# Norm weights applied to the transposed x, as a scale of its high and low parts, and first loads in halves

## The reference

```python
def rms_norm(x, g):
    y = x32 * lax.rsqrt(jnp.mean(x32 * x32, axis=-1, keepdims=True) + EPS)
    return (y * g).astype(x.dtype)

x = x + 0.5 * swiglu_ffn(x, ffn1_norm, ffn1_w_in, ffn1_w_out)   # D_FF = 5632
h = rms_norm(x, mix_norm)
proj = h @ w_in                                                 # six parts: q, k, v for A and for B
...                       # per-head norms, rotary, 8 dilated heads, 8 differential heads
x = x + mixed @ w_out
x = x + 0.5 * swiglu_ffn(x, ffn2_norm, ffn2_w_in, ffn2_w_out)
```

## Time and profile before

| | us |
|---|---|
| median of 3 runs | 1875.55 (1874.54 to 1876.12) |
| the profiled execution, whole | 1874.67 |
| its span in the profile | 1872.9 |
| PE busy | 1851.4 (99% of the span) |
| DVE busy | 1271.5 (68%) |
| ACT busy | 936.4 (50%) |

### The profile page before, as it was taken

One profiled execution on the slowest core, in us unless ns is written; L12 is line 12 of the kernel. 1 busy time (PEld: TensorE's weight loads), 2 busy tenths in 40 slices (PEclk: granted clock), 3 DMA queues, 4 the chain that ended last, 5 costly groups with the idle time before them and its releaser, 6 DMA issues.

```text
span 1872.9 us, 23158 instructions
## 1 busy us (share of the span) xinstructions
PE 1851.4 (99%) x8408; PEld 1531.9 (82%) x8408; DVE 1271.5 (68%) x1432; ACT 936.4 (50%) x1167; POOL 60.1 (3%) x60
## 2 busy tenths in 40 slices
PE   7999999999999999999999999999999999999999
PEld 6888888888888888877888788888888888888887
DVE  6777788778754554668777667688877887744443
ACT  5455555555543444555555555555555555533432
POOL 0000000000000000222021100000000000000000
PEclk9999999999999999999999999999999999999999
DMA  8555555555655555554545445455555555555563
GB/s 291 189 191 209 192 199 205 193 188 179 231 196 175 184 196 198 188 181 135 180 157 180 135 157 180 157 200 198 207 197 206 183 209 191 201 180 180 193 212 113
DMA packets 178137, 352.88 MB, mean 188 GB/s; under 512 B 6561, under 2 KB 7201, under 8 KB 177825
## 3 DMA queue, kind: packets, MB, share of 16 engines
q1 hardware_dynamic: 177936, 352.07, 54.7%
q10 hardware_dynamic: 144, 0.07, 0.0%
HBM read 350.01 MB, written 2.10 MB: 188 GB/s over the span
## 4 chain that ended last, share of the span: by engine, by line
PE 94%; DVE 3%; ACT 1%; issue 1%; POOL 1%; DMA 1%; SPq 0%; ACTq 0%
PE acc L376 21%; PE acc L378 20%; PE acc L377 20%; PE acc L480 6%; PE acc L481 6%; PE acc L479 6%; PE turn L419 2%; PE turn L420 2%; PE turn L418 2%; DVE w_lo L874 2%; PE turn L403 1%; PE acc L420 1%; PE acc L418 1%; PE acc L419 1%; PE turn L531 1%
## 5 line engine op out<-in xcount | busy, mean ns | idle before, releaser
L874 DVE TENSOR_TENSOR w_lo<-w_raw,w_hi 128x1024 fp32r<-128x1024 f32 x352 | 428.8, 1229 | 392.4 <-ACT w_hi L634 390.5
L634 ACT ACTIVATE w_hi<-w_raw 128x1024 fp32r<-128x1024 f32 x352 | 357.6, 1020 | 461.9 <-PE acc L378 440.2
L648 ACT ACTIVATE w_hi<-w_raw 128x1024 fp32r<-128x1024 f32 (+1 forms) x400 | 402.9, 1017 | 363.7 <-PE acc L481 131.5
L883 DVE TENSOR_TENSOR w_lo<-w_raw,w_hi 128x1024 fp32r<-128x1024 f32 (+1 forms) x400 | 460.6, 1169 | 151.9 <-ACT w_hi L648 146.3
L376 PE MATMUL acc<-w_hi,h_hi 128*128 128x512 f32 x992 | 392.4, 396 | 1.9 <-DVE w_lo L874 1.9
L378 PE MATMUL acc<-w_hi,h_lo 128*128 128x512 f32 x992 | 387.5, 391 | 0.0
L377 PE MATMUL acc<-w_lo,h_hi 128*128 128x512 f32 x992 | 387.3, 390 | 0.0
L376 PE MATMUL acc<-w_hi,act_hi 128*128 128x512 f32 x704 | 278.0, 395 | 0.0
L378 PE MATMUL acc<-w_hi,act_lo 128*128 128x512 f32 x704 | 276.0, 392 | 0.0
L377 PE MATMUL acc<-w_lo,act_hi 128*128 128x512 f32 x704 | 273.7, 389 | 0.0
L376 PEld LDWEIGHTS acc<-w_hi,h_hi 128*128 128x128 f32 x992 | 186.8, 188 | 42.1 <-issue 4.9
(11 more groups left out here) (133 smaller groups left out, 1571.7 us busy)
## 6 DMA issues: line engine op xcount, KB each, us to landing
w_raw<-in_ffn_w_in SPq DMA_DIRECT2D x176, 1024.0 KB, 4.9
w_raw<-in_ffn_w_out SPq DMA_DIRECT2D x64, 1024.0 KB, 5.0
w_raw<-in_w_in SPq DMA_DIRECT2D x48, 1024.0 KB, 5.1
w_raw<-in_ffn_w_out SPq DMA_DIRECT2D x32, 768.0 KB, 4.2
w_raw<-in_w_out SPq DMA_DIRECT2D x16, 1024.0 KB, 5.0
x_sb<-in_x SPq DMA_DIRECT2D x4, 512.0 KB, 7.9
out_y<-x_sb SPq DMA_DIRECT2D x4, 512.0 KB, 6.4
gain_row<-in_ffn_norm SPq DMA_DIRECT2D x4, 256.0 KB, 8.6
```

The lines of the kernel that those rows point to most:

```text
L634: nc.scalar.activation(w_hi[:, v % RING, 0:count, :], w_raw[:, v // 2 % RAW, k0:k0 + count, :], ACT.Copy).then_inc(hi_ready, 1)
L648: nc.scalar.activation(w_hi[:, v % RING, 0:count, :], w_raw[:, piece % RAW, k0:k0 + count, :], ACT.Copy).then_inc(hi_ready, 1)
L874: nc.vector.tensor_tensor(w_lo[:, v % RING, 0:count, :], w_raw[:, v // 2 % RAW, k0:k0 + count, :], w_hi[:, v % RING, 0:count, :].bitcast(F32),
L883: nc.vector.tensor_tensor(w_lo[:, v % RING, 0:count, :], w_raw[:, piece % RAW, k0:k0 + count, :], w_hi[:, v % RING, 0:count, :].bitcast(F3 ...
```

## The change

The norm weights are no longer broadcast. ACT's queue loads the three vectors as 48 rows of 128 (`norm_in`), PE transposes them once, and ACT copies them into `norm_gain`, one value per partition and tile. PE transposes x itself (`turn_x`, `turn_norm`), and the weight is applied while the result is split: ACT copies with a scale (`turn_norm_hi`), DVE forms x times weight minus the high part (`norm_lo`). As the scale differs from tile to tile, a group of 512 columns takes four instructions of 256 elements on each of the two engines, instead of one of 1024. `gain_x`, `gain_row` and its loads are gone, six in number. The first 256 columns of x and the first two tiles of weights are loaded by themselves, before the rest of their groups. Group 1 is transposed after unit 0, group 2 after unit 2, group 3 after unit 4. The squares of x are later in ACT's stream, and `down` is written out for its four chunks in place of a loop.

```diff
-            for c in range(4):
+            first = gate_up1[:, 0:UK, 0:NC], gate_up1[:, UK:2 * UK, 0:NC]
+            sp.dma_start(x_sb[:, :, 0:NC // 2], x_dram[:, :, 0:NC // 2]).then_inc(x_half_landed, 16)
+            sp.dma_start(w_raw[:, 0, 0:UK, :], first[0]).then_inc(first_landed, 16)
+            sp.dma_start(x_sb[:, :, NC // 2:NC], x_dram[:, :, NC // 2:NC]).then_inc(x_landed[0], 16)
+            sp.dma_start(w_raw[:, 0, UK:2 * UK, :], first[1]).then_inc(raw_landed[0], 16)
+            for c in range(1, 4):
                 cols = slice(c * NC, (c + 1) * NC)
                 sp.dma_start(x_sb[:, :, cols], x_dram[:, :, cols]).then_inc(x_landed[c], 16)
-                sp.dma_start(gain_row[:, cols], ffn1_norm[:, cols].to_broadcast([P, NC])).then_inc(x_landed[c], 16)
-                if c:
-                    load(gate_up1, 0, KT * (c - 1), KT, c - 1)
-            load(gate_up1, 0, KT * 3, KT, 3)
+                load(gate_up1, 0, KT * c, KT, c)
...
+            def turn_x(c, pair, split, ks=range(4)):
+                if split is not None:
+                    pe.wait_ge(turn_split, split)
+                for k in ks:
+                    for t in range(TT):
+                        at = c * NC + k * P
+                        mm = nc.tensor.transpose(turn4[pair][:, k, t * P:(t + 1) * P], x_sb[:, t, at:at + P], ident)
+                return mm
...
-                    chunk(PARTS_D, u0, range(1), h, 0, r0 - 4)
-                    turn_rows(r0 - 2, xg_at[2], r0 - 3)
-                    chunk(PARTS_D, u0, range(1, 4), h, 0, r0 - 4)
+                    pe.wait_ge(half_split, 1)
+                    chunk(PARTS_D, u0, range(1), h, 0)
+                    pe.wait_ge(x_landed[1], 16)
+                    turn_norm(1, xg_at[1], None)
+                    pe.wait_ge(turn_split, 1)
+                    chunk(PARTS_D, u0, range(1, 3), h, 0, r0 - 4)
+                    pe.wait_ge(x_landed[2], 16)
+                    turn_norm(2, xg_at[2], r0 - 3)
+                    chunk(PARTS_D, u0, range(3, 5), h, 0, r0 - 4)
+                    pe.wait_ge(x_landed[3], 16)
+                    turn_norm(3, xg_at[3], r0 - 2)
+                    chunk(PARTS_D, u0, range(5, 8), h, 0, r0 - 4)
...
+            def turn_norm_hi(n, r, c, pair):
+                act.wait_ge(rows_turned, r + 1)
+                for k in range(4):
+                    s = nc.scalar.activation(h_hi[:, 4 * c + k, :], turn4[pair][:, k, :], ACT.Copy,
+                                             scale=norm_gain[:, n, 4 * c + k:4 * c + k + 1])
+                s.then_inc(turn_hi, 1)
...
+            def norm_lo(n, c, pair, ks):
+                for k in ks:
+                    at = 4 * c + k
+                    s = nc.vector.scalar_tensor_tensor(h_lo[:, at, :], turn4[pair][:, k, :], norm_gain[:, n, at:at + 1],
+                                                       h_hi[:, at, :].bitcast(F32), ALU.mult, ALU.subtract)
+                return s
...
-            for c in range(2):
-                dve.wait_ge(x_landed[c], 32)
-                gain_x(ROWS[R_NORM1] + c, c, 0)
...
+            norm_lo(0, 0, xg_at[0], range(0, 2)).then_inc(half_split, 1)
+            split_lo(IN1, 0, 1, PARTS_D)
+            dve.wait_ge(turn_hi, 1)
+            norm_lo(0, 0, xg_at[0], range(2, 4)).then_inc(turn_split, 1)
+            split_lo(IN1, 1, 2, PARTS_D)
+            turn_norm_lo(0, 1, 1, xg_at[1])
+            split_lo(IN1, 2, 4, PARTS_D)
+            turn_norm_lo(0, 2, 2, xg_at[2])
+            split_lo(IN1, 4, 6, PARTS_D)
+            turn_norm_lo(0, 3, 3, xg_at[3])
```

More of the change, by code:

```diff
@@ L174, in hybrid_layer_kernel @@
             head_rstd = sb("head_rstd", [P, TT * HEADS_C], F32, attention)
+            norm_in = sb("norm_in", [3 * KD, P], F32, attention)
             lam_in = sb("lam_in", [P, 4, SUB], F32, attention)
@@ L483, in hidden, with down @@
                     mm.then_inc(units_used, 1)
[L485 to L495, removed]
-                    pe.wait_ge(turn_split, r0 + FFN_ITERS)
-                    chunk(PARTS_F, u0, range(20, UNITS_F), act, b)
+            def down(s_out, c, r0, turns):
+                u0, b = UNIT[s_out] + c * UNITS_F, c % 2
+                bank_wait(s_out, b, c // 2)
+                chunk(PARTS_F, u0, range(4), act, b)
+                if c == 0:
+                    turn_rows(R_FFN1 if s_out == OUT1 else R_FFN2, r0 + FFN_ITERS - 1, 0, r0 + FFN_ITERS - 1)
+                elif turns:
+                    wait_read(pe, s_out, c - 1)
+                    turn_norm(c - 1, xg_at[c - 1], r0 + FFN_ITERS + (c - 1 if c > 1 else 0))
+                chunk(PARTS_F, u0, range(4, 20), act, b)
+                pe.wait_ge(turn_split, r0 + FFN_ITERS)
+                chunk(PARTS_F, u0, range(20, UNITS_F), act, b)
             def ffn(s_in, s_out, r0, n, final):
@@ L502, in ffn @@
                     hidden(s_in, i, r0, n)
-                if final:
-                    down(s_out, 0, r0, 1)
-                    down(s_out, 1, r0, 0)
-                else:
-                    with pe.Fori(0, 2) as i:
-                        down(s_out, i, r0, 2)
+                for c in range(4):
+                    down(s_out, c, r0, not final)
             def turn_qk(u):
@@ L596, in _ @@
             pe.wait_ge(ident_landed, 16)
-            for c in range(2):
-                turn_rows(ROWS[R_NORM1] + c, xg_at[c], None)
+            pe.wait_ge(norm_landed, 48)
+            nc.tensor.transpose(turn[0][:, 0:3 * KD], norm_in[:, :], ident[0:3 * KD, 0:3 * KD]).then_inc(norm_turned, 1)
+            pe.wait_ge(x_half_landed, 16)
+            turn_x(0, xg_at[0], None, range(0, 2)).then_inc(half_turned, 1)
+            pe.wait_ge(x_landed[0], 16)
+            turn_x(0, xg_at[0], None, range(2, 4)).then_inc(rows_turned, 1)
+            pe.wait_ge(norm_ready, 1)
             ffn(IN1, OUT1, ROWS[R_FFN1], 0, False)
@@ L682, in hidden, with ffn @@
                 split_in_hi(s_in, i, n, 18, 24)
-            def ffn(s_in, s_out, r0, n, updated, final):
-                split_hi(s_in, 4, 6, PARTS_D)
-                updated()
-                square_x(2 * n, 3)
-                split_hi(s_in, 6, 8, PARTS_D)
-                turn_split_hi(r0 - 1, h_hi, 12, 0)
+            def ffn(s_in, s_out, r0, n, final):
+                if n:
+                    split_hi(s_in, 4, 6, PARTS_D)
+                    wait_read(act, PROJ, 3)
+                    square_x(2, 3)
+                split_hi(s_in, 6, 8, PARTS_D)
+                if n:
+                    turn_norm_hi(2, r0 - 1, 3, 0)
+                else:
+                    for c in (2, 3):
+                        act.wait_ge(x_landed[c], 16)
+                        square_x(0, c)
                 split_hi(s_in, 8, 9, PARTS_D)
                 act.wait_ge(turn_split, r0)
-                nc.scalar.activation(rows[:, 1, 0, :].rearrange("p (k s) -> p k s", s=SEQ), turn4[0][:, 0:UK, :],
-                                     ACT.Copy).then_inc(half_copied, 1)
+                for k in range(4):
+                    s = nc.scalar.activation(rows[:, 1, k // 2, k % 2 * SEQ:(k % 2 + 1) * SEQ], turn4[0][:, k, :],
+                                             ACT.Copy, scale=norm_gain[:, 2 * n, 12 + k:13 + k])
+                s.then_inc(half_copied, 1)
                 split_hi(s_in, 9, 10, PARTS_D)
@@ L976, in activation_sums @@
             def activation_sums(n):
-                x_1 = rows[:, 1, 0, :].rearrange("p (k s) -> p k s", s=SEQ)
-                a_11, a_21 = x_1[:, :, 0:P], x_1[:, :, P:2 * P]
-                a_12, a_22 = turn4[0][:, UK:2 * UK, 0:P], turn4[0][:, UK:2 * UK, P:2 * P]
+                h_4 = rows[:, 1, :, :].rearrange("p t (k s) -> p t k s", s=SEQ)
+                (a_11, a_21), (a_12, a_22) = ((h_4[:, b, :, 0:P], h_4[:, b, :, P:2 * P]) for b in range(2))
                 sums = rows[:, 0, :, :].rearrange("p t (g k s) -> p (t g) k s", g=2, k=UK)
@@ L1036, in ffn @@
                     update_x(s_out, c, UNITS_F * (c + 1), 0.5)
-                    if not final:
-                        if c == 0:
-                            dve.wait_ge(gain_landed, 16)
-                        gain_x(r + 1, c, r)
             def lambda_sums():
```

145 lines of the change are left out of this document (77 added, 68 removed).

## The result

The changed kernel took **1894.79 us** (median; 1889.55 to 1895.67), the kernel before 1875.51 us in the same comparison. The ratio is 1.0102, with a 95% interval of 1.0091 to 1.0113. The forecast of 1878.8 us had the right sign but 16 us too little, and the time lies outside its range. The profiled execution took 1895.36 us, with a span of 1893.6.

The account below looks back on a forecast made before the run. PE, busy 99% of the span, was taken as the bound. Start -4.5, clock +0.9, transposes +0.9 and three new waits +6.0 gave +3.3 us on 1874.67 (1878.0; 1878.9 from the median); forecast 1878.8, range 1875.5 to 1885.0.

Follow-up runs that it names:

- b_pad128: The kernel before with an unused buffer of 128 bytes per partition ahead of `act` and `mix`: 1885.28 us, ratio 1.0055.
- b_pad64: The kernel before with an unused buffer of 64 bytes per partition ahead of `act` and `mix`: 1868.47 us, ratio 0.9968.
- b_hshift_2: The kernel before with `h_hi` and `h_lo` alone moved to 192 beyond a multiple of 256, discarded squares as 8-bit floats: 1902.81 us, ratio 1.0147.
- a_whole: The changed kernel with one whole copy and subtraction per column group 1 to 3 of x in the first norm, weights left out there: 1888.48 us, ratio 1.0071.
- a_place: The changed kernel with `act` and `mix` put back at the addresses of the kernel before, discarded squares as 8-bit floats: 1883.32 us, ratio 1.0038.
- a_early: The changed kernel with the earlier transpose order, `act` and `mix` at 139136, first norm's vector loaded before the identity, x's group 1 issued earlier: 1864.05 us, ratio 0.9939.

## What to carry to other kernels

When PE sets the time, compare its pace in stages that the diff does not touch: the span from one landmark to the next with the same count of instructions. A stage that slows down with no wait and at full clock may have another layout, as it did here, and an unused buffer of 64 or 128 bytes tests that in one run, also as the control of any edit that adds or resizes a buffer. When work moves between engines, count the units of cover for the whole chain and not for one engine, and price a wait of PE near 2 us at nearly twice its length, as the three here cost 5.9 us and 4.8 more.

## What the runs showed of the hardware

- The pace of these float32 matmuls (128x128 stationary, 512 columns) depends on the distance between the start of the stationary operand's buffer and the moving one's, modulo 256 bytes: 0 is best, 192 costs 2.2 ns, 128 costs 5.6 and 64 costs 6.6 per matmul of about 0.23 us. In this kernel that is up to 0.9% of the time for `act` and `mix` (`b_pad128` against `b_pad64`), and 1.5% for `h` (`b_hshift_2`).
- PE waits of 1.0 us left the granted clock at 1.00 (`a_whole`); waits of 2.0 us were followed by seven or eight matmuls at the lower level in both traces that have them (changed kernel, `a_place`). By their mean clocks a few executions seem to have been spared.
- On ACT's queue, while SP's queue loaded x and weights, the identity of 64 KB landed 3.2 us after its issue as the first transfer and 4.9 us after it as the second (`a_early`). The three vectors of 8 KB behind it in the changed kernel took 3.2, 4.1 and 5.3 us.
